# A decoder layer: the memory values computed in plain fp32 from weights read in place, and a third place for the old residual

## The reference

```python
def mem_kv(mem, p):
    m = rms_norm(mem, p['g_mem'])          # mem: 1 x 256 x 1024
    k = (m @ p['w_xk']).reshape(B, N, X_HEADS, X_HEAD_DIM)
    v = (m @ p['w_xv']).reshape(B, N, X_HEADS, X_HEAD_DIM)
    return k, v

def layer(...):
    m, ... = token_mixer(rms_norm(x, p['g_pre_mix']), ...)   # ends in: concat(attn, cv) @ p['w_out']
    x = x + rms_norm(m, p['g_post_mix'])
    xa = cross_attend(rms_norm(x, p['g_pre_x']), mem_k, mem_v, p)
```

## Time and profile before

| | |
|---|---|
| median of 3 runs | 2034.86 us (2034.53 to 2036.19) |
| profiled execution, its own time | 2033.87 us |
| span of the profiled execution, first to last instruction | 2032.0 us |
| TensorE busy in the span | 1857.1 us (91%) |
| VectorE, ScalarE, GpSimd busy | 1174.8, 481.8, 589.3 us |
| mean granted TensorE clock | 0.970 |

### The profile page before, as it was taken

The page is one execution under the profiler, slowest core; times in us unless marked ns, Lnnn a source line. Parts: engine busy times, 40 slices in busy tenths (PEclk is TensorE's granted clock), DMA queues, the critical chain, the costliest instruction groups (busy, mean ns, idle before and its releaser), DMA issues. The chain is left out here.

```text
span 2032.0 us, 27594 instructions
## 1 busy us (share of the span) xinstructions
PE 1857.1 (91%) x10840; PEld 1657.8 (82%) x10840; DVE 1174.8 (58%) x1665; ACT 481.8 (24%) x810; POOL 589.3 (29%) x437
## 2 busy tenths in 40 slices
PE   6998888699999899899859989999999999999995
PEld 6998554356667898788729879999999999999983
DVE  7886599866665337333323797445454554545547
ACT  4021332144444423222222341001100100110011
POOL 3331489710000124321013722223222322232220
PEclk9999899799999999999989989999999999999997
DMA  5214422100000214400451211111111111111102
GB/s 160 99 42 58 173 94 94 32 31 1 1 1 1 85 48 156 144 21 10 164 213 52 94 42 42 42 41 41 51 42 41 41 51 42 41 41 49 44 14 88
DMA packets 42715, 128.42 MB, mean 63 GB/s; under 512 B 12464, under 2 KB 18736, under 8 KB 40016
## 3 DMA queue, kind: packets, MB, share of 16 engines
q1 hardware_dynamic: 39984, 105.17, 15.7%
q0 software_dynamic: 1792, 18.88, 2.4%
q10 hardware_dynamic: 864, 3.34, 0.5%
HBM read 118.81 MB, written 8.56 MB: 63 GB/s over the span
## 5 line engine op out<-in xcount | busy, mean ns | idle before, releaser
L252 POOL CAST w_hi<-raw 128x1024 fp32r<-128x1024 f32 x90 | 98.0, 1088 | 811.3 <-issue 319.7
L281 PE MATMUL ps<-xo_hi,w_hi 128*128 128x384 f32 (+1 forms) x1248 | 292.5, 332 | 18.3 <-DVE xo_lo L2644 6.2
L281 PE MATMUL ps<-xo_lo,w_hi 128*128 128x384 f32 (+1 forms) x1248 | 290.5, 331 | 0.0
L281 PE MATMUL ps<-xo_hi,w_lo 128*128 128x384 f32 (+1 forms) x1248 | 289.9, 330 | 0.0
L281 PEld LDWEIGHTS ps<-xo_hi,w_hi 128*128 128x128 f32 x1248 | 218.1, 189 | 22.2 <-issue 13.2
L254 POOL TENSOR_TENSOR w_lo<-raw,w_hi 128x1024 fp32r<-128x1024 f32 x90 | 221.1, 2456 | 7.2
L281 PEld LDWEIGHTS ps<-xo_lo,w_hi 128*128 128x128 f32 x1248 | 218.7, 190 | 0.2
L281 PEld LDWEIGHTS ps<-xo_hi,w_lo 128*128 128x128 f32 x1248 | 218.3, 189 | 0.0
L2597 DVE TENSOR_TENSOR xo<-ps,xo 128x768 f32<-128x768 f32 (+1 forms) x160 | 108.4, 719 | 130.6 <-PE ps L281 130.6
L377 DVE SCALAR_TENSOR_TENSOR x<-u_prompt,vecs,x 128x1024 f32<-128x1024 f32 x120 | 164.7, 1373 | 3.4
L2549 DVE TENSOR_TENSOR ffn_g_prompt<-ffn_g_prompt,ffn_rstd 128x1024 f32<-128x1024 f32 x22 | 67.4, 3062 | 167.2 <-ACT ffn_g_sample L2414 167.2
(11 more groups left out here) (348 smaller groups left out, 3352.6 us busy)
## 6 DMA issues: line engine op xcount, KB each, us to landing
raw<-in_units SPq DMA_DIRECT2D x128, 512.0 KB, 3.3
xs_keys<-in_cache_k_t SPq DMA_DIRECT2D x8, 1024.0 KB, 8.3
xs_vals<-in_cache_v_t SPq DMA_DIRECT2D x16, 512.0 KB, 13.3
x<-in_x_t SPq DMA_DIRECT2D x8, 544.0 KB, 9.3
out_y_t<-x SPq DMA_DIRECT2D x2, 1792.0 KB, 6.6
out_old<-in_x_t ACTq DMA_DIRECT2D x6, 544.0 KB, 4.0
mla_wq<-in_w_q_t SPq DMA_DIRECT2D x1, 1536.0 KB, 8.3
out_kv_latent_t<-c SPq DMA_DIRECT2D x1, 1088.0 KB, 13.0
```

The costliest lines, as they stand in the source:

```text
L252: nc.gpsimd.tensor_copy(K.w_hi[:, s, :], K.raw[:, s, :]).then_inc(K.hi_done[s], 1)
L281: mm = nc.tensor.matmul(out(at, n), w, x(k, at, n), start=first and k == 0 and p == 0, stop=last and k == len(tiles) - 1 and p == 2)
```

## The change

The values are computed as the keys were: plain fp32, from the raw weights, with `mem_whole`. So `mem_hi`, `mem_lo`, their instructions and GpSimd's `split_values` are gone; GpSimd only counts `hi_done` and `split_done` up by eight for both places. Both places of the raw weights are now loaded again only when TensorE has used them, in order, and the load of the next stage's pair waits for the last use of both. `OLD` is 3 instead of 2. The core of the diff:

```diff
-        OLD = 2
+        OLD = 3
...
-        mem_hi, mem_lo = (sb(f"mem_{x}", [P, KD, N_MEM], F32R) for x in ("hi", "lo"))
...
             for p in range(base + OUT_PAIRS, base + OUT_PAIRS + KV_PAIRS):
-                sp.wait_ge(K.split_done[1], p)
-                sp.dma_start(K.raw[:, 1, :], K.A.units[2 * p + 1]).then_inc(K.unit_in[1], 16)
-                sp.wait_ge(K.split_done[0], p)
-                sp.wait_ge(used[0], p)
-                sp.dma_start(K.raw[:, 0, :], K.A.units[2 * p]).then_inc(K.unit_in[0], 16)
-            sp.wait_ge(used[0], base + OUT_PAIRS + KV_PAIRS)
+                for s in range(2):
+                    sp.wait_ge(K.split_done[s], p)
+                    sp.wait_ge(used[s], p)
+                    sp.dma_start(K.raw[:, s, :], K.A.units[2 * p + s]).then_inc(K.unit_in[s], 16)
+            for s in range(2):
+                sp.wait_ge(used[s], base + OUT_PAIRS + KV_PAIRS)
             load_units(sp, K, 1, OUT_PAIRS + KV_PAIRS - 1)
...
-            def split_values(j):
...
             split(K.fed, base + OUT_PAIRS)
-            for j in range(KV_PAIRS):
-                split_values(j)
+
+            for s in range(2):
+                pool.wait_ge(K.split_done[s], base + OUT_PAIRS)
+                for _ in range(KV_PAIRS):
+                    pool.sem_inc(K.hi_done[s], 1)
+                    pool.sem_inc(K.split_done[s], 1)
             split(base + OUT_PAIRS + KV_PAIRS, K.fed + OUT_PAIRS + KV_PAIRS)
...
             def memory_unit(u):
                 s, j = u % 2, OUT_PAIRS + u // 2
-                if s == 0:
-                    pe.wait_ge(K.unit_in[s], 16 * (base + j + 1))
-                else:
-                    pe.wait_ge(K.split_done[s], base + j + 1)
+                pe.wait_ge(K.unit_in[s], 16 * (base + j + 1))
                 if u >= 4:
                     pe.wait_ge(kv_out, u - 3)
-                if s == 0:
-                    for k in range(KD):
-                        mm = nc.tensor.matmul(kv_acc(u), K.raw[:, s, k * P:(k + 1) * P], mem_whole[:, k, :],
-                                              start=k == 0, stop=k == KD - 1)
-                else:
-                    mm = accumulate(nc, K, lambda at, n: kv_acc(u)[:, at:at + n], u // 2 % 2,
-                                    lambda k, at, n: mem_hi[:, k, at:at + n], lambda k, at, n: mem_lo[:, k, at:at + n],
-                                    chunks=[(0, N_MEM)])
+                for k in range(KD):
+                    mm = nc.tensor.matmul(kv_acc(u), K.raw[:, s, k * P:(k + 1) * P], mem_whole[:, k, :], start=k == 0,
+                                          stop=k == KD - 1)
                 mm.then_inc(used[s], 1)
...
-            pe.wait_ge(mem_made, KD)
+            pe.wait_ge(mem_scaled, KD)
...
-            for k in range(KD):
-                act.wait_ge(mem_scaled, k + 1)
-                nc.scalar.activation(mem_hi[:, k, :], mem_whole[:, k, :], ACT.Identity).then_inc(mem_hi_made, 1)
...
-            def mem_low(k):
-                dve.wait_ge(mem_hi_made, k + 1)
-                nc.vector.tensor_tensor(mem_lo[:, k, :], mem_whole[:, k, :], mem_hi[:, k, :].bitcast(F32),
-                                        ALU.subtract).then_inc(mem_made, 1)
```

More of the change, by code:

```diff
@@ L1492, in out_stage @@
             sem(x) for x in ("hi_made", "lo_made", "m_out", "squared", "summed", "total_ready", "rooted", "rstd_ready"))
-        mem_in, mem_squared, mem_summed, mem_total, mem_rooted, mem_rstd, mem_scaled, mem_hi_made, mem_made = (
+        mem_in, mem_squared, mem_summed, mem_total, mem_rooted, mem_rstd, mem_scaled = (
             sem(x) for x in ("mem_in", "mem_squared", "mem_summed", "mem_total", "mem_rooted", "mem_rstd",
-                             "mem_scaled", "mem_hi_made", "mem_made"))
+                             "mem_scaled"))
         old_in = [sem(f"old_in{r}") for r in range(OLD)]
@@ L1543, in split @@
                                                 ALU.subtract).then_inc(K.split_done[s], 1)
-            def split_values(j):
[L1547 to L1550, removed]
-                else:
[L1552 to L1559, removed]
-            split(K.fed, base + OUT_PAIRS)
-            for j in range(KV_PAIRS):
-                split_values(j)
+            split(K.fed, base + OUT_PAIRS)
+            for s in range(2):
[3 more added lines that the diff above has]
+                    pool.sem_inc(K.split_done[s], 1)
             split(base + OUT_PAIRS + KV_PAIRS, K.fed + OUT_PAIRS + KV_PAIRS)
@@ L1705, in _ @@
                                      scale=1.0 / D_MODEL).then_inc(rooted, 1)
-            act.wait_ge(mem_made, KD)
+            act.wait_ge(mem_scaled, KD)
             for j in range(KV_PAIRS):
@@ L1763, in _ @@
                                                ALU.mult, ALU.mult).then_inc(mem_scaled, 1)
-                if k >= 1:
-                    mem_low(k - 1)
-            mem_low(KD - 1)
             for u in range(4, KD):
```

## The result

The changed kernel takes 2044.79 us (median of 5 runs) against 2036.19 for the kernel before in the same comparison: a ratio of 1.0041, 95% interval [1.0028, 1.0054]. By that ratio it is 8.4 us slower (8.6 by the two medians), between 5.7 and 11.0. The forecast was 7.2 us slower. The profiled execution has a span of 2041.6 us, 9.6 more than before.

The account below looks back on a forecast made before the run. The prediction took TensorE's order of work to bound this stage. Its terms, +4.6 - 1.1 - 5.4 + 5.2 + 3.9, gave +7.2 us and a median of 2042.1, own range 2039 to 2044.5.

Parts of the forecast that it names:

- Work of the value units: Memory part on TensorE: eight value units become plain fp32, 3.45 us each instead of 2.87, +4.6 us.
- the working of before: TensorE's work in the kernel before, from unit 1 to behind unit 15: 52.8 of 58.23 us, the rest waits.
- VectorE's sum: VectorE's last sum of squares, which TensorE waits for, shortens from 2.41 to 1.29 without GpSimd's value splits: -1.1 us.
- The waits for weights: TensorE's memory units: old waits for loads go, -5.4 us; new ones come as places free only after use, +5.2.
- the single collisions: After units 3 and 5, a weight load behind one old-residual load of ScalarE: a wait of 0.8 us each.
- The double one: After unit 7, a weight load meeting two old-residual loads of ScalarE: a wait of 2.6 us.
- The other nine starts: Starts of memory units just as their weight load lands, put at 0.1 us each: 1.0 in all.
- The tail: Unit 15's end to the next stage: the next pair loads later and GpSimd's split loses its cover, 7.6 to 11.5, +3.9 us.
- Halves and third place: Removing the memory halves' copies and subtractions, and a third old-residual load at the stage's start: both cost nothing.
- range of all cases: The forecast time's range over all cases, 2037 to 2046.5 us, up to full collisions with scatter.
- the clock fell in a gap: Sign of being wrong: loads take so long that TensorE's clock falls in the gaps; no size given.
- every collision in full: Rival, chance 0.14: singles go half way to 6.81, the double all the way; waits 9 for 5.2, +11, 2045.9 us.

Follow-up runs that it names:

- four_places: The changed kernel with two more raw places in the room of the halves and the next pair loaded after units 12 and 13: ratio 0.9982 to the kernel before.
- no_reload: The changed kernel without ScalarE's five loads of the old residual: ratio 1.0017 to the kernel before.
- old2: The changed kernel with two places for the old residual instead of three, so six loads by ScalarE: ratio 1.0049 to the kernel before.
- late_pair: The kernel before, with SyncE loading the next stage's pair only after the last use of both places: ratio 1.0019 to the kernel before.
- no_store: The changed kernel without the stores of the memory keys and values and the wait for them: ratio 1.0041 to the kernel before.
- early_place: The changed kernel with the next pair's first place loaded after unit 14 again, the second after unit 15: ratio 1.0037 to the kernel before.
- old5: The changed kernel with five places for the old residual, so three loads by ScalarE: ratio 1.0037 to the kernel before.

## Why the prediction was right, step by step

**Work of the value units, +4.6.** Right. 6.91 for two units, as the row of before gave it. Without waits units 1 to 15 take 57.67 (four_places), where the working of before had 52.8: 4.9 more, 4.6 of it the units.

**VectorE's sum, -1.1.** Right: 1.29 instead of 2.41, and TensorE's idle time in front of its sums 0.24 instead of 1.37. That it was GpSimd, bear out: its subtraction ended at 772.05 and VectorE's sum at 773.19, 1.14 later, nearly the whole time that the sum takes alone. From unit 0 to unit 1 the gain is 0.88 (5.79 against 6.67).

**The waits for weights, -5.4 and +5.2.** The mechanism was right and shown by no_reload; the size of the new waits was low, 6.4 for 5.2. 65.79 less 57.67 is 8.1, of which 1.7 is the clock in this execution and 6.4 the waits. The term that was mis-sized is that of the single collisions: I put them at 0.8, and behind units 3 and 5 they cost 1.3 and 2.0 (788.31 to 789.78 and 796.80 to 799.04, less 0.2 for the transposes). The double one, put at 2.6, cost 1.9, no more than the single one behind unit 5. The other nine starts, put at 1.0 together, cost 1.2, but not as foreseen: 0.9 of it is one wait, before unit 3. It came without a reload in flight, and was between 0 and 0.9 in the kernels with reloads and two raw places. The rate of the transfers from 776.9 to 784.0 us, in 40 slices of 0.18 us, shows how that load, issued at 777.01, ended:

```profile
GB/s 0 92 0 0 0 0 208 162 115 300 415 462 392 369 254 116 23 23 23 23 23 23 23 46 0 185 138 69 208 300 369 392 415 369 369 139 0 0 0 0
```

The bulk had moved by 779.7, and a rest then went at 23 GB/s for over 1 us. In old2, where the wait is missing, so is this rest. What makes it stays open. The Trainium skill ("DMA: Bandwidth & Descriptors", Issuing engines are not separate DMA queues) says that transfers begun by different engines run on the same 16 DMA engines and interleave. The trace agrees: beside the reloads of ScalarE's queue SyncE's loads took up to 5.4, and without them, in no_reload, 3.5 at most.

**The tail, +3.9.** Right in kind, and 4.5 in size (late_pair, the same step alone: 4.3). Most of the 0.6 is the first load, which was there for GpSimd after 4.3 instead of 3.87. The working let the store be 3 later and still land in time; it took 8.4 instead of 4.1, behind the late loads, and landed only 0.3 before the splits were through. no_store shows that the splits are enough for a tail of 11.70, early_place that the store is next in line at 9.75.

**Halves and third place, 0.** Right for the halves: from the stage's first transfer (666.30, before 666.81) to unit 0 are 101.2 us, where it was 101.5. The third place is worth the one wait of 1.7 that old2 has more; the prediction had it in its count of five reloads.

**The sum.** In the stage, 11.2 (83.67 against 72.49): 4.6 from the units, -0.9 before unit 1, 3.0 from waits and clock against those of before, 4.5 from the tail. That is 4.0 over the forecast: 1.7 in the clock, 1.2 in the waits, 0.6 in the tail, and 0.5 in VectorE's sum and the units, all to the same side. The span grew by 9.6, since the rest of the kernel was 1.6 shorter in this execution, and the runs by 8.4 [5.7, 11.0]. So the causes were right, but that the runs came so near to 7.2 is in part luck. The median, 2044.79, lies 0.3 above the prediction's own range and inside its range of all cases; 1.3 of its distance from 2042.1 is the kernel before, which took 2036.19 here and 2034.86 there.

One of the prediction's signs of being wrong did come: the clock fell in a gap. The prediction had no price for it, and it cost 1.7 in this execution. The waits don't depend on it: early_place, no_store, old2 and old5 show them at a granted clock of 1.00. Of the rivals, "every collision in full" (+11) has the size of the stage's 11.2, but by coincidence: it put the waits at 9 and the double collision above the single ones, and the 6.4 measured are nearer to the forecast's 5.2.

## What to carry to other kernels

When a buffer's release moves from its copy to its last use, the load has just one unit's time; ask for it alone, and then with every other load that is issued at the same event. Work that a neighbour's last unit was covering (here the split of the next pair, and the store behind its load) must be followed to the barrier, not only to its own engine. Room that a change frees is worth using: two more places, with the next pair loaded early again, turned a loss of 0.4% into a gain of 0.2%.

## What was not expected of the hardware

After an idle gap of 1.87 us before 799.04 the granted clock went to its lower level in the changed kernel (means of 0.72 and then 0.50 over 2 us each), and two units took 1.7 longer. In no_store a gap of 1.91 before unit 9 left it at 1.00, and so did in early_place a gap of 1.82 before 800.74:

```profile
799.00:801.00 2.00, 0.27 (x1) 0.27 (x2) 1.69 (x2) 0.39 (x2) 0.00 (x0) 1.00 0.99 358
801.00:803.00 2.00, 2.00 (x11) 1.74 (x11) 0.00 (x0) 0.00 (x0) 0.00 (x0) 1.00 0.22 88
```

ScalarE's queue starts a reload before the activations that stand in front of it in the program. Behind unit 7 of the changed kernel, tile 2's reload comes before its two activations, and tile 3's before tile 2's second one:

```profile
804.50 0.36 ACTq L1659 DMA_DIRECT2D out_old<-in_x_t  x1
804.77 1.19 ACT L1653 ACTIVATE hx_hi<-x,vecs 128x1088 fp32r<-128x1088 f32 x1
804.96 0.40 ACTq L1659 DMA_DIRECT2D out_old<-in_x_t  x1
805.86 1.10 ACT L1657 ACTIVATE out_sq<-x 128x1088 f32<-128x1088 f32 x1
```

The last wait in front of the first one is that of ScalarE's copy of unit 7 for the end of that unit; the copy began at 804.49. SyncE's load waits for the same event. So both reloads meet it:

```profile
804.53 0.33 SPq L1520 DMA_DIRECT2D raw<-in_units  x1
```

Two of them, 0.46 us apart, cost TensorE little more than one.
